# Decoding the picked experts with integers, and starting the gate groups one unit earlier

## The chip, the cores and the metric

The kernel runs on one core of one Trainium2 chip. The metric is the device time of one execution in microseconds (us), the median of the runs shown. The engines are named PE (TensorE), DVE (VectorE), ACT (ScalarE), POOL (GpSimd) and SP (SyncE, here only a DMA queue).

## The reference, cut to what matters

Two transformer blocks in fp32 over 256 tokens of width 2048. The change lies in the expert layer (PEER) of the first block:

```python
q = (t @ wq).reshape(T, 8, 2, 128)
s1, s2 = q[:, :, 0] . k1, q[:, :, 1] . k2            # 128 scores per head and half
v1, i1 = top_k(s1, 16);  v2, i2 = top_k(s2, 16)
cand = (v1[..., :, None] + v2[..., None, :])         # 16 x 16 sums
sc, pos = top_k(cand, 16)                            # slot = pos // 16, pos % 16
idx = i1[slot // 16] * 128 + i2[slot % 16]
g = softmax(sc)
out = sum_k g_k * gelu(u[idx_k] . t) * v[idx_k]
```

There are 8 heads with 16 picks each, so 128 picks a token. For each pick the kernel has a position of 0 to 255 in the 16 x 16 table; its upper four bits are a slot in the first list of keys, its lower four a slot in the second. Looking up which key (0 to 127) stands in that slot is called decoding here.

## The kernel before, in words

**The weight stream.** All large weights come as one stream of 532 units of 128x2048 fp32, loaded by SP into four raw buffers. Each unit is split into two fp32r parts so that PE keeps nearly fp32 precision: ACT copies it rounded (`w_hi`, line 672, the function `ahead` of ACT) and DVE subtracts that from the raw unit (`w_lo`, line 1117, `ahead` and `lo` of DVE). There are two buffers of each. ACT may write unit k+2 only when PE has finished unit k (`mm_done`); DVE may subtract only when ACT has written; PE may begin a unit only when DVE has subtracted (`split_done`). The next raw load into a slot starts when its unit is split. `ahead(u)` on ACT and on DVE prepares unit u+2.

**The expert layer.** It is computed densely for 208 of the 256 tokens. The first stages of the stream are `wq` (16 units, queries), `u0` and `u1` (16 units each, the scores of the experts 0 to 2047 and 2048 to 4095), then `e0` and `e1` (their outputs), and so on. A unit of `u0` or `u1` is 48 matmuls of 208 columns (lines 1884 to 1886). Beside `wq` and `u0` DVE does the top-k searches, and after them the decoding, lines 1482 to 1506, in which it places a `fill()` between its own steps: a `fill()` is the DVE half of `ahead` for the next unit of `u0`. For each half of the tokens (`tt`) DVE casts the key numbers to floats (`top_f`), cuts the positions into two slots (`posab`), casts those (`posf`), and then for each of the two lists (`half`) compares the slots with 0 to 15 (line 1499), multiplies the result by the key numbers (line 1502) and adds up over 16 (line 1506). Two more `fill()` follow, since six of the sixteen were placed in the search and eight in the decoding.

**The gates.** The softmax is begun by DVE (line 1492, `sm_dve`), its exponentials are ACT's (line 900). In ACT's order of work they stand behind all of `u0`, so behind the eviction of its last unit and behind the copy of `w_hi` for the second unit of `u1`. DVE then divides (lines 1511 to 1513) and signals `picks_done`. PE turns the picks by six transposes (`picks_turn`, line 2192), DVE copies them (lines 1523 and 1524) and builds one-hot tiles: for a gate group of four tokens `picks(q)` writes one `pick_b` (line 1532) and four `pick_a` (line 1537). PE multiplies them (`gate_group`, line 2203), ACT evicts the group into `stage` (line 909), and every fourth group is written to memory (line 913) and partly kept (line 916). There are 52 groups. `picks(q)` waits for the matmuls of group q-2. `GATES_UNIT` says which unit of `u1` holds which groups: five each in the units 1 to 10, two in unit 11. Within a unit PE puts them behind the steps kt = 2, 5, 8, 11 and 15 of its 16 (`GATES_AFTER`). DVE puts the `w_lo` of unit k+1 behind the second group of unit k. ACT, in unit k, evicts up to four groups, then waits for the end of the unit, evicts it with a Gelu (line 925), copies `w_hi` of unit k+2, and evicts the fifth group.

**Behind the gates.** When the last group is evicted, DVE weighs the activations of `u0` by the gates, four tiles at a time (`gated0`, lines 1555, 1567, 1570). `gated0(0)` also waits until the last even block of gates is written to memory. Only then comes the next `w_lo`, and after it `gated0(1)` and so on. Stage `e0` begins when all 16 units of `u1` are done.

Of the kernel before, what the change touches and what calls it, by code (L numbers as in the profile page):

```python
# [15 lines left out]
F32 = mybir.dt.float32  # L16
F32R = mybir.dt.float32r
U32 = mybir.dt.uint32
ACT = mybir.ActivationFunctionType
AX = mybir.AxisListType  # L20

P = 128
# [13 lines left out]
PEER_HEADS, PEER_KEYS, TOPK = 8, 128, 16  # L36
PICKS = PEER_HEADS * TOPK
# [90 lines left out]
def build(nc, x_in, mem_in, stream, cols_in, consts_in, rows_in, wide_in, wdtf_in, keys_in,  # L128
          rel_in, onehot_in, u_rows, v_rows, out):
    ctx = ExitStack()  # L130
    with ctx:
        base = [-(-nc.sbuf_base // 32) * 32]

        def at(name, shape, dt, offset):
            return nc.alloc_sbuf_tensor_at(name, shape, dt, offset=offset)
# [25 lines left out]
        work_at = base[0]  # L161
# [27 lines left out]
        def C(name, a=0, b=None):  # L189
            lo, hi = CONSTS[name]  # L190
            return consts[:, lo + a:(hi if b is None else lo + b)]
# [24 lines left out]
        act0 = at("act0", [P, KT, T], F32, work_at)  # L216
        wide = at("wide", [P, D], F32, work_at)
        cand = at("cand", [P, 2, TT, 256], F32, work_at + 24576)
        onehot = at("onehot", [P, PICKS, TOPK], F32, work_at + 24576)
        pick_a = at("pick_a", [P, 8, P], F32, work_at + 24576)  # L220
        pick_b = at("pick_b", [P, 8, P], F32, work_at + 28672)
        gbuf = at("gbuf", [P, 4, TBLOCKS, 4 * TBLOCK], F32, work_at + 16384)
        pk = work_at + 32768

        top_v = [at(f"top_v{tt}", [P, 16, TOPK], F32, o) for tt, o in enumerate((pk, wdtf_at))]
        top_i = [at(f"top_i{tt}", [P, 16, TOPK], U32, o + 1024) for tt, o in enumerate((pk, wdtf_at))]
        top_f = at("top_f", [P, 16, TOPK], F32, pk + 2048)
        sc = at("sc", [P, TT, PEER_HEADS, TOPK], F32, pk + 3072)
        pos = [at(f"pos{tt}", [P, PEER_HEADS, TOPK], U32, pk + o) for tt, o in enumerate((4096, 12928))]
        posab = at("posab", [P, 2, PICKS], U32, pk + 4608)  # L230
        posf = at("posf", [P, 2, PICKS], F32, pk + 5632)
        picked = at("picked", [P, TT, 3, PICKS], F32, pk + 6656)
        pickT = at("pickT", [P, 3, T], F32, pk + 9728)
        gsum = at("gsum", [P, TT, PEER_HEADS], F32, pk + 12800)
# [188 lines left out]

        GROUPS = TD // 4
        GATES_AFTER = (2, 5, 8, 11, 15)
        GATES_UNIT = {1 + q // 5: [n for n in range(GROUPS) if n // 5 == q // 5] for q in range(GROUPS)}

        LAST_GROUP = max(GATES_UNIT)

# [236 lines left out]
        def _(act):  # L666
# [253 lines left out]
            for k in range(16):  # L920
                u, groups = UNIT0["u1"] + k, GATES_UNIT.get(k, [])
                for q in groups[:4]:
# [187 lines left out]
        def _(dve):  # L1110
            eng = nc.vector
            own = Steps(eng, dve_own)
# [7 lines left out]
            def ahead(u, *loops):  # L1120
                lo(lin(u + 3, *loops), u + 2)
# [227 lines left out]
            for s in range(MIX_STEPS):  # L1349
# [11 lines left out]
                n = s - SSD_AT  # L1361
# [95 lines left out]
            waiting = [UNIT0["u0"] + j for j in range(16)]  # L1457

            def fill():
                ahead(waiting.pop(0))  # L1460
# [3 lines left out]
            for s in range(2 * PEER_HEADS + 6):  # L1464
                for k in range(2):
                    one, two = KEYS_AT.get(s - 1 - k), KEYS_AT.get(s - 3 - k)
# [11 lines left out]
                if s == 2:  # L1478
                    eng.wait_ge(s_wide2, 16)
                    eng.tensor_tensor(xw[0:G, :], x[0:G, 0, :], wide2[0:G, :], ALU.mult).then_inc(xw_done, 1)  # L1480

            for tt in range(TT):
                own.did(eng.tensor_copy(top_f[:, :, :], top_i[tt][:, :, :]))
                tf = top_f[:, :, :].rearrange("p (h two) k -> p h two k", two=2)

                own.did(eng.tensor_copy(first[:, :], sc[:, tt, :, 0]))

                pf = pos[tt][:, :, :].rearrange("p h k -> p (h k)")
                own.did(eng.tensor_scalar(posab[:, 0, :], pf, 4, None, ALU.logical_shift_right))
                own.did(eng.tensor_scalar(posab[:, 1, :], pf, 15, None, ALU.bitwise_and))  # L1490
                own.wait()
                eng.tensor_tensor(sc[:, tt, :, :], sc[:, tt, :, :],
                                  first[:, :].unsqueeze(2).to_broadcast([P, PEER_HEADS, TOPK]),
                                  ALU.subtract).then_inc(sm_dve, 1)
                own.do(eng.tensor_copy(posf[:, :, :], posab[:, :, :]))
                for half in range(2):
                    if waiting:
                        fill()
                    own.do(eng.tensor_tensor(onehot[:, :, :], C("iota", 0, TOPK).unsqueeze(1).to_broadcast([P, PICKS, TOPK]),
                                             posf[:, half, :].unsqueeze(2).to_broadcast([P, PICKS, TOPK]), ALU.is_equal))  # L1500
                    oh = onehot[:, :, :].rearrange("p (h k) a -> p h k a", h=PEER_HEADS)
                    own.do(eng.tensor_tensor(oh, oh, tf[:, :, half, :].unsqueeze(2).to_broadcast([P, PEER_HEADS, TOPK, TOPK]),
                                             ALU.mult))
                    if waiting:
                        fill()
                    own.do(eng.tensor_reduce(picked[:, tt, half, :], onehot[:, :, :], AX.X, ALU.add))
            while waiting:
                fill()
            for tt in range(TT):
                eng.wait_ge(sm_act, tt + 1)  # L1510
# [26 lines left out]
                    eng.tensor_scalar(pick_a[:, j + i, :], C("iota"), pickT[:, 0, t:t + 1], pickT[:, 2, t:t + 1],  # L1537
                                      ALU.is_equal, ALU.mult).then_inc(oha_done, 1)

            for k in range(1, LAST_GROUP + 1):  # L1540
                for n, q in enumerate(GATES_UNIT[k]):
                    if n == min(2, len(GATES_UNIT[k]) - 1):
                        ahead(UNIT0["u1"] + k - 1)
                    picks(q)
# [325 lines left out]
        def _(pe):  # L1870
            eng = nc.tensor
# [294 lines left out]
            for s in range(WQ_STEPS):  # L2166
                if s in KEYS_AT:
                    h = KEYS_AT[s]
# [17 lines left out]
            def picks_turn():  # L2186

                eng.wait_ge(picks_done, TT)
                for n in range(3):
                    for tt in range(TT):  # L2190
                        o = bank[6 + n // 2][:, (n % 2) * T + tt * P:(n % 2) * T + tt * P + P]
                        last = eng.transpose(o, picked[:, tt, n, :], C("ident"))
                last.then_inc(pickT_psum, 1)

            def gate_group(q):

                eng.wait_ge(ohb_done, q + 1)
                if q >= 4:
                    eng.wait_ge(g_evict, q - 3)
                for i in range(4):  # L2200
                    eng.wait_ge(oha_done, 4 * q + i + 1)
                    j = 4 * (q % 2) + i
                    mm(bank[4 + q % 4][:, i * P:i * P + P], pick_b[:, j, :], pick_a[:, j, :], start=True, stop=True)\
                        .then_inc(g_mm, 1)

            for k in range(16):
                groups = GATES_UNIT.get(k, [])

                def between(kt, groups=groups):
                    if kt in GATES_AFTER and GATES_AFTER.index(kt) < len(groups):  # L2210
                        gate_group(groups[GATES_AFTER.index(kt)])

                eng.wait_ge(split_done, UNIT0["u1"] + k + 1)
                eng.wait_ge(bank_free, 4 * ROUND0["u1"] + k + 1)
                if k == 1:
                    picks_turn()
                feature_unit(k, a1, between=between, c0=G)
            feature("e0", 16, None, unit=part_unit, tile=e0_pair, c1=TD, ready=lambda kt: eng.wait_ge(a2_ready, Z_TILES + kt + 1))
# [145 lines left out]
            for j in range(8, 16):  # L2364
# [5 lines left out]
                if j in (8, 9, 12):  # L2370
                    n = {8: 0, 9: 1, 12: 2}[j]
# [169 lines left out]
```

## Time and profile before

| what | value |
|---|---|
| time, median of 3 runs | 3111.43 us (3110.13 to 3116.72) |
| the profiled execution | 3117.25 us, of which the span of the profile is 3115.5 us |
| busy share of the span | PE 97%, DVE 72%, ACT 46%, POOL 6% |
| mean granted clock of PE | 0.99 of 2.4 GHz |
| `u0` ends, picks turned, first `pick_b` | 644.2, 650.6, 652.6 us |
| last `pick_a` ends, `e0` begins | 762.8, 789.1 us |

Times in the rows are microseconds from the start of the span. A row of a timeline gives start, duration, engine, line, operation, output<-input, shape, count, and in brackets the idle time of the engine before it with what ended that. A row of the stretches gives, for each engine, busy time and (instructions), and then the granted clock of PE as a share of 2.4 GHz, the busy share of the DMA engines and GB/s.

### The profile page before, as it was taken

What the parts mean: (1) busy time and instruction counts of PE and PEld (TensorE: products, weight loads), DVE (VectorE), ACT (ScalarE), POOL (GpSimd) and SP (SyncE); (2) the same over time, 40 slices, a digit from 0 to 9 for tenths busy, and PEclk for the clock granted to TensorE, in tenths of its full rate; (3) what the DMA queues carried; (4) which work ended last, traced back from release to release, by engine and by line L of the source; (5) the groups of instructions that cost most, each with busy time, mean ns of one, the idle gap of its engine ahead of it and who ended that gap; (6) DMA issues with size and microseconds to landing.
All of it is one profiled execution on the core that took longest, in us unless ns stands there. A gap on an engine that the chain in (4) does not pass through costs nothing. (4 is left out here: it accounts for less than half of the span.)

```text
span 3115.5 us, 49787 instructions
## 1 busy us (share of the span) xinstructions
PE 3019.5 (97%) x19428; PEld 2808.5 (90%) x19428; DVE 2258.5 (72%) x3201; ACT 1426.0 (46%) x1762; POOL 180.1 (6%) x223
## 2 busy tenths in 40 slices
PE   7999999999997999999999999999999999999998
PEld 7899889999997999999999999999788888888886
DVE  4766559999865889888988877598656646555564
ACT  4465443356443444555454455434444333333333
POOL 1000000020000111111111100000000000000000
PEclk9999999999998999999999999999999999999999
DMA  5443464456768999999999874544444555555553
GB/s 204 175 149 136 150 211 150 166 199 229 255 252 227 339 343 354 342 352 343 356 338 359 315 294 179 182 177 150 162 176 148 185 194 188 189 188 188 188 188 135
DMA packets 101661, 705.49 MB, mean 226 GB/s; under 512 B 13320, under 2 KB 13344, under 8 KB 17728
## 3 DMA queue, kind: packets, MB, share of 16 engines
q1 hardware_dynamic: 77472, 562.07, 50.0%
q0 software_dynamic: 22192, 128.10, 11.9%
q10 hardware_dynamic: 1872, 13.63, 1.1%
q8 instruction: 80, 1.31, 0.2%
q14 instruction: 45, 0.37, 0.0%
HBM read 685.46 MB, written 18.24 MB: 226 GB/s over the span
## 5 line engine op out<-in xcount | busy, mean ns | idle before, releaser
L1117 DVE TENSOR_TENSOR w_lo<-raw,w_hi 128x2048 fp32r<-128x2048 f32 x532 | 1218.5, 2290 | 514.8 <-ACT w_hi L672 489.6
L1906 PE MATMUL bank<-a_both,w_hi 128*128 128x416 f32 (+1 forms) x3840 | 1231.0, 378 | 25.5 <-DVE w_lo L1117 21.8
L1907 PE MATMUL bank<-a_both,w_lo 128*128 128x208 f32 (+1 forms) x4096 | 1042.8, 265 | 0.0
L1906 PEld LDWEIGHTS bank<-a_both,w_hi 128*128 128x128 f32 x3840 | 725.5, 189 | 80.9 <-issue 25.7
L1907 PEld LDWEIGHTS bank<-a_both,w_lo 128*128 128x128 f32 x4096 | 782.6, 191 | 7.2
L672 ACT ACTIVATE w_hi<-raw 128x2048 fp32r<-128x2048 f32 x308 | 588.4, 1911 | 379.8 <-PE bank L1938 361.6
L1884 PE MATMUL bank<-a_both,w_hi 128*128 128x256 f32 (+1 forms) x1984 | 572.9, 289 | 21.0 <-DVE w_lo L1117 13.7
L685 ACT ACTIVATE w_hi<-raw 128x1536 fp32r<-128x1536 f32 x224 | 333.7, 1490 | 523.2 <-PE bank L1907 503.7
L1885 PE MATMUL bank<-a_both,w_hi 128*128 128x256 f32 (+1 forms) x1984 | 560.0, 282 | 0.0
L1886 PE MATMUL bank<-a_both,w_lo 128*128 128x256 f32 (+1 forms) x1984 | 559.9, 282 | 0.0
L1884 PEld LDWEIGHTS bank<-a_both,w_hi 128*128 128x128 f32 x1984 | 383.7, 193 | 28.9 <-issue 11.1
L1885 PEld LDWEIGHTS bank<-a_both,w_hi 128*128 128x128 f32 x1984 | 383.9, 193 | 0.5
L1886 PEld LDWEIGHTS bank<-a_both,w_lo 128*128 128x128 f32 x1984 | 383.5, 193 | 0.0
L1936 PE MATMUL bank<-w_hi,a_both 128*128 128x512 f32 x960 | 377.6, 393 | 2.0 <-DVE a_both L1128 1.5
L1938 PE MATMUL bank<-w_hi,a_both 128*128 128x512 f32 x960 | 373.9, 389 | 0.0
L1937 PE MATMUL bank<-w_lo,a_both 128*128 128x512 f32 x960 | 373.6, 389 | 0.0
L1936 PEld LDWEIGHTS bank<-w_hi,a_both 128*128 128x128 f32 x960 | 180.2, 188 | 40.6 <-DVE a_both L1128 2.2
L1938 PEld LDWEIGHTS bank<-w_hi,a_both 128*128 128x128 f32 x960 | 180.2, 188 | 37.9
L1937 PEld LDWEIGHTS bank<-w_lo,a_both 128*128 128x128 f32 x960 | 180.3, 188 | 36.3
L1906 PE MATMUL bank<-e_both,w_hi 128*128 128x416 f32 x480 | 146.0, 367 | 0.0
L691 ACT ACTIVATE w_hi<-raw 128x512 fp32r<-128x512 f32 x224 | 138.3, 617 | 0.0
L1907 PE MATMUL bank<-e_both,w_lo 128*128 128x208 f32 x512 | 127.1, 258 | 0.0
(327 smaller groups left out, 2529.3 us busy)
## 6 DMA issues: line engine op xcount, KB each, us to landing
raw<-stream_dram SPq DMA_DIRECT2D x532, 1024.0 KB, 4.9
gates_scratch<-stage ACTq DMA_DIRECT2D x13, 1024.0 KB, 4.4
gbuf<-gates_scratch POOLq DMA_DIRECT2D x30, 416.0 KB, 7.3
x<-x_dram SPq DMA_DIRECT2D x2, 1024.0 KB, 6.5
x_scratch<-x POOLq DMA_DIRECT2D x1, 2048.0 KB, 11.0
set_rows<-xw_scratch POOLq DMA_DIRECT2D x2, 1024.0 KB, 22.9
mem<-mem_dram POOLq DMA_DIRECT2D x1, 2048.0 KB, 9.7
xm<-x_scratch POOLq DMA_DIRECT2D x1, 2048.0 KB, 12.5
```

The lines of the kernel that those rows point to most:

```text
L672: eng.activation(w_hi[k % SPLIT][:, :], raw[:, k % RAW, :], ACT.Copy).then_inc(hi_done, 1)
L685: eng.activation(w_hi[k % SPLIT][:, 0:PART], raw[:, k % RAW, 0:PART], ACT.Copy)
L691: eng.activation(w_hi[k % SPLIT][:, PART:UNIT], raw[:, k % RAW, PART:UNIT], ACT.Copy).then_inc(hi_done, 1)
L1117: eng.tensor_tensor(w_lo[k % SPLIT][:, :], raw[:, k % RAW, :], w_hi[k % SPLIT][:, :].bitcast(F32), ALU.subtract).then_inc(split_done, 1)
L1884: mm(o, hi[:, ks], tile(0, kt), start=kt == 0, stop=False)
L1885: mm(o, hi[:, ks], tile(1, kt), start=False, stop=False)
L1886: last = mm(o, lo[:, ks], tile(0, kt), start=False, stop=kt == KT - 1)
L1906: mm(o, hi[:, ks], pair, start=kt == 0, stop=False)
L1907: inst = mm(o2, lo[:, ks], pair[:, 0, :], start=False, stop=False, skip_group_check=True)
L1936: mm(o, tile(0, k0 + k)[:, ts], hi[:, ns], start=first and k == 0, stop=False)
L1937: mm(o, tile(0, k0 + k)[:, ts], lo[:, ns], start=False, stop=False)
L1938: last = mm(o, tile(1, k0 + k)[:, ts], hi[:, ns], start=False, stop=end and k == 3)
```

## The change

The decoding is done in integers. Each key number gets its own slot number above it (`slot * 128` or'ed on, `top_x`), the slots wanted are shifted left by seven bits in the instruction that cuts them out, and an exclusive-or of the two gives the bare key number where the slots agree and at least 128 where they don't; a minimum over sixteen leaves the key number. So the multiplication over 2048 elements and the cast `posf` fall away, and one small instruction that makes the slot numbers comes in.

The gate groups begin one unit earlier: three in unit 0 of `u1` (behind kt = 8, 11, 15), five each in the units 1 to 9, four in unit 10. The picks are turned ahead of unit 0 instead of unit 1. One `fill()` is left over in `waiting` and never taken from it: the `w_lo` of unit 1 of `u1` is now written behind the second gate group, by the loop over the groups, which starts at k = 0.

```diff
-        onehot = at("onehot", [P, PICKS, TOPK], F32, work_at + 24576)
+        differ = at("differ", [P, PICKS, TOPK], U32, work_at + 24576)
-        top_f = at("top_f", [P, 16, TOPK], F32, pk + 2048)
+        top_x = at("top_x", [P, 16, TOPK], U32, pk + 2048)
-        posf = at("posf", [P, 2, PICKS], F32, pk + 5632)
+        slot_x = at("slot_x", [P, TOPK], U32, pk + 5632)
...
-        GATES_UNIT = {1 + q // 5: [n for n in range(GROUPS) if n // 5 == q // 5] for q in range(GROUPS)}
+        GATES_UNIT = {(q + 2) // 5: [n for n in range(GROUPS) if (n + 2) // 5 == (q + 2) // 5] for q in range(GROUPS)}
...
+            own.do(eng.tensor_scalar(slot_x[:, :], C("iota", 0, TOPK), float(PEER_KEYS), None, ALU.mult))
             for tt in range(TT):
-                own.did(eng.tensor_copy(top_f[:, :, :], top_i[tt][:, :, :]))
-                tf = top_f[:, :, :].rearrange("p (h two) k -> p h two k", two=2)
+                own.did(eng.tensor_tensor(top_x[:, :, :], top_i[tt][:, :, :],
+                                          slot_x[:, :].unsqueeze(1).to_broadcast([P, 16, TOPK]), ALU.bitwise_or))
+                tx = top_x[:, :, :].rearrange("p (h two) k -> p h two k", two=2)
...
-                own.did(eng.tensor_scalar(posab[:, 0, :], pf, 4, None, ALU.logical_shift_right))
-                own.did(eng.tensor_scalar(posab[:, 1, :], pf, 15, None, ALU.bitwise_and))
+                own.did(eng.tensor_scalar(posab[:, 0, :], pf, 4, 7, ALU.logical_shift_right, ALU.logical_shift_left))
+                own.did(eng.tensor_scalar(posab[:, 1, :], pf, 15, 7, ALU.bitwise_and, ALU.logical_shift_left))
...
-                own.do(eng.tensor_copy(posf[:, :, :], posab[:, :, :]))
                 for half in range(2):
                     if waiting:
                         fill()
-                    own.do(eng.tensor_tensor(onehot[:, :, :], C("iota", 0, TOPK).unsqueeze(1).to_broadcast([P, PICKS, TOPK]),
-                                             posf[:, half, :].unsqueeze(2).to_broadcast([P, PICKS, TOPK]), ALU.is_equal))
-                    oh = onehot[:, :, :].rearrange("p (h k) a -> p h k a", h=PEER_HEADS)
-                    own.do(eng.tensor_tensor(oh, oh, tf[:, :, half, :].unsqueeze(2).to_broadcast([P, PEER_HEADS, TOPK, TOPK]),
-                                             ALU.mult))
+                    own.do(eng.tensor_tensor(
+                        differ[:, :, :].rearrange("p (h k) a -> p h k a", h=PEER_HEADS),
+                        posab[:, half, :].rearrange("p (h k) -> p h k", h=PEER_HEADS).unsqueeze(3)
+                        .to_broadcast([P, PEER_HEADS, TOPK, TOPK]),
+                        tx[:, :, half, :].unsqueeze(2).to_broadcast([P, PEER_HEADS, TOPK, TOPK]), ALU.bitwise_xor))
                     if waiting:
                         fill()
-                    own.do(eng.tensor_reduce(picked[:, tt, half, :], onehot[:, :, :], AX.X, ALU.add))
-            while waiting:
+                    own.do(eng.tensor_reduce(picked[:, tt, half, :], differ[:, :, :], AX.X, ALU.min))
+            while len(waiting) > 1:
                 fill()
...
-            for k in range(1, LAST_GROUP + 1):
+            for k in range(LAST_GROUP + 1):
...
-                def between(kt, groups=groups):
-                    if kt in GATES_AFTER and GATES_AFTER.index(kt) < len(groups):
-                        gate_group(groups[GATES_AFTER.index(kt)])
+                places = GATES_AFTER if k else GATES_AFTER[-len(groups):]
+
+                def between(kt, groups=groups, places=places):
+                    if kt in places and places.index(kt) < len(groups):
+                        gate_group(groups[places.index(kt)])
...
-                if k == 1:
+                if k == 0:
                     picks_turn()
```

## Rows read from the trace of the kernel before

**Rows 1.** The page: busy time of each engine over the span.
```profile
PE 3019.5 (97%) x19428; PEld 2808.5 (90%) x19428; DVE 2258.5 (72%) x3201; ACT 1426.0 (46%) x1762; POOL 180.1 (6%) x223
```

**Rows 2.** The stretches: the gates, and from the last group to `e0`.
```profile
651.20:762.10 110.90, 104.26 (x909) 102.46 (x907) 109.47 (x271) 77.95 (x84) 17.74 (x36) 1.00 0.59 218
762.10:789.10 27.00, 25.99 (x230) 25.85 (x231) 22.00 (x55) 9.95 (x10) 7.00 (x6) 1.00 0.87 278
```

**Rows 3.** The timeline of DVE: one half of the decoding and its cast.
```profile
591.68 0.28 DVE L1495 CAST posf<-posab 128x256 f32<-128x256 uint32 x1
...
596.42 2.28 DVE L1499 TENSOR_TENSOR onehot<-consts,posf 128x2048 f32<-128x2048 f32 x1
598.74 2.29 DVE L1502 TENSOR_TENSOR onehot<-onehot,top_f 128x2048 f32<-128x2048 f32 x1
601.07 2.29 DVE L1117 TENSOR_TENSOR w_lo<-raw,w_hi 128x2048 fp32r<-128x2048 f32 x1
603.27 2.28 DVE L1506 TENSOR_REDUCE picked<-onehot 128x128 f32<-128x2048 f32 x1
```

**Rows 4.** The timeline of ACT: evictions of units 7, 8 and 15 of `u0`.
```profile
597.33 0.34 ACT L894 ACTIVATE act<-bank 128x208 f32<-128x208 f32 x1 [3.22 <-PE bank L1886]
...
602.68 0.34 ACT L894 ACTIVATE act<-bank 128x208 f32<-128x208 f32 x1 [3.21 <-PE bank L1886]
...
644.48 0.34 ACT L894 ACTIVATE act<-bank 128x208 f32<-128x208 f32 x1 [3.87 <-PE bank L1886]
```

**Rows 5.** The timeline of PE: the longest of five late unit starts.
```profile
627.46 0.36 PE L1884 MATMUL bank<-a_both,w_hi 128*128 128x208 f32 x1 [1.25 <-DVE w_lo L1117]
```

**Rows 6.** The timeline of ACT behind that eviction: the exponentials.
```profile
644.72 1.91 ACT L672 ACTIVATE w_hi<-raw 128x2048 fp32r<-128x2048 f32 x1
646.64 1.28 ACT L900 ACT_TABLE_LOAD   x1
647.94 0.51 ACT L900 ACTIVATE sc<-sc 128x128 f32<-128x128 f32 x2
```

**Rows 7.** The timeline of DVE: softmax, copies, first two groups.
```profile
648.87 0.28 DVE L1511 TENSOR_REDUCE gsum<-sc 128x8 f32<-128x128 f32 x1
...
651.50 0.69 DVE L1523 COPY pickT<-bank 128x512 f32<-128x512 f32 x1 [0.58 <-PE bank L2192]
...
652.55 0.69 DVE L1532 TENSOR_TENSOR pick_b<-consts,pickT 128x512 f32<-128x512 f32 x1
...
654.18 0.69 DVE L1532 TENSOR_TENSOR pick_b<-consts,pickT 128x512 f32<-128x512 f32 x1
```

**Rows 8.** The timeline of PE: the turn of the picks.
```profile
650.61 0.85 PE L2192 MATMUL bank<-consts,picked 128*128 128x128 f32 x6 [0.81 <-DVE picked L1513]
```

**Rows 9.** The timeline of PE: a longer wait.
```profile
560.75 0.54 PE L1884 MATMUL bank<-a_both,w_hi 128*128 128x208 f32 x1 [2.88 <-DVE w_lo L1117]
```

**Rows 10.** The stretch behind this wait, and one behind another wait.
```profile
560.70:566.70 6.00, 5.95 (x28) 5.96 (x29) 5.93 (x21) 0.00 (x0) 0.00 (x0) 0.50 0.50 178
...
1932.30:1935.40 3.10, 3.10 (x16) 3.10 (x16) 3.10 (x3) 0.00 (x0) 0.00 (x0) 0.50 0.74 259
```

**Rows 11.** The timeline of ACT: one group is evicted.
```profile
660.31 1.06 ACT L909 ACTIVATE stage<-bank 128x512 f32<-128x512 f32 x1 [2.47 <-PE bank L2203]
```

**Rows 12.** The timeline of DVE behind the last group.
```profile
761.66 1.11 DVE L1537 TENSOR_SCALAR pick_a<-consts,pickT 128x128 f32<-128x128 f32 x4
765.14 1.23 DVE L1555 TENSOR_TENSOR act<-act,gbuf 128x208 f32<-128x208 f32 x4 [2.37 <-ACT gbuf L916]
768.65 0.80 DVE L1567 CAST e_both<-act 128x208 fp32r<-128x208 f32 x4 [2.27 <-DMA gates_scratch<-stage]
...
770.63 2.28 DVE L1117 TENSOR_TENSOR w_lo<-raw,w_hi 128x2048 fp32r<-128x2048 f32 x1
```

**Rows 13.** The timeline of PE: unit 13 of `u1`, and the first matmul of `e0`.
```profile
772.97 0.37 PE L1884 MATMUL bank<-a_both,w_hi 128*128 128x208 f32 x1 [0.96 <-DVE w_lo L1117]
...
789.14 0.42 PE L1906 MATMUL bank<-e_both,w_hi 128*128 128x416 f32 x1
```

## The prediction

> **What bounds the kernel now.** The page comes first: PE is busy for 97% of the span [rows 1], so a change on DVE pays only where PE waits for DVE. The stretches come next: between the turn of the picks and the last gate group DVE is busy for 109.5 of 110.9 us [rows 2], so there DVE sets the pace and PE waits a little in each unit. Then the timelines around the change. In the decoding the unit starts of `u0` are late: an unhindered unit takes 5.35 us (597.33 to 602.68), but the last seven take 41.8 us (602.68 to 644.48) instead of 37.4 [rows 4]. So 4.4 us are lost, in five late starts, the longest of which waits 1.25 us for `w_lo` [rows 5]. Behind the last group the chain is another: group evicted, written to memory, activations weighed, and only then the next `w_lo` [rows 12]. The view of ACT matters as well: the exponentials come behind the last unit's eviction and a `w_hi` [rows 6].
>
> **The change, step by step.** The sum is made against the profiled execution (3117.25 us, span 3115.5); that is 5.8 us over the median of 3111.43, and I carry the difference over to the median.
>
> *Decoding.* Four multiplications of 2.29 us fall away with their gaps (598.74 to 601.07, 2.33 each), so 9.3 us, and two casts of about 0.3 [rows 3]; one small instruction (0.2) comes in. DVE has 9.7 us less to do. The exclusive-or over 2048 uint32 is not in the trace, nor is the minimum. I take the 2.28 us of the comparison and of the sum, of the same shape. Lower bound: 1.9 us, ACT's pass over 2048 [rows 6], which changes nothing, as will be seen; upper bound: 4.6 us, as much as comparison and multiplication together [rows 3]. The or over 256 elements and the double shifts go by the cast and by the instructions that they replace, a tenth more or less.
> What it is worth: per two units of `u0` DVE then has two `w_lo` (2 x 2.2) and two passes (2 x 2.3), 9.0 us against PE's 10.7. The late starts go, PE is the bound, and the last eviction moves from 644.48 to 640.1: **-4.4 us**. More cannot come of it, for a faster DVE now waits for `w_hi`. About half of the 9.7 us ends as idle time.
>
> *The turn of the picks.* It now stands ahead of unit 0 of `u1`, so PE has nothing to do from the end of `u0` until `picks_done`. From the last eviction to the first exponential done it is 3.8 us (644.48 to 648.2), which doesn't shrink [rows 6]: 643.9. From DVE's `gsum` to the turn it is 1.74 us (648.87 to 650.61) [rows 7, 8]: the turn starts at 645.7 (650.61 before), after 5.6 us without work on PE; before, unit 0 filled this time and the wait was 0.81 [rows 8]. A wait of 2.88 us was followed by 6.0 us at a granted clock of 0.50, another by at least 3.1 [rows 9, 10]; so after 5.6 us I expect the 1.2 GHz level for 3.1 to 6 us, middle 4.7, in which PE loses half. The six transposes then take 0.5 more. First `pick_b`: 645.7 + 1.9 + 0.5 = 648.1 against 652.55 [rows 7], again **-4.4**.
>
> *The groups of unit 0.* From here to the last `pick_a` (762.77) DVE did 52 groups of 1.63 and eleven `w_lo` [rows 7, 12]; now it is the same number, unit 1's in place of unit 12's. What is added is idle time. The `w_hi` of unit 2 waits on ACT behind three evictions, the third of a group that PE reaches only behind kt = 15. DVE has the first five groups and one `w_lo` out at 648.1 + 8.2 + 2.2 = 658.5, of which 0.5 is held back by PE's matmuls at most. The third group ends on PE near 657.1; eviction 1.1 [rows 11], table load 1.3, Gelu 0.3, `w_hi` 1.9 [rows 6]: 661.7. DVE stands for 2.7 us. PE then waits 3.4 us for group 5, the clock falls a second time, and DVE waits some 2.0 us for slow matmuls (`picks` stays within two groups of PE). With 0.2 of the 0.5, idle time is 4.9 us where it was 1.1: **+3.8**. The last `pick_a` ends 0.6 us earlier than before, at 762.2.
>
> *Behind the last group.* Before, the `w_lo` that follows the weighing was unit 13's: 762.77 to the unit's start at 772.97 is 10.2 us, with 0.96 of wait, and three units lead to `e0` at 789.14 [rows 12, 13]. Now the last group is in unit 10, and the `w_lo` behind the same chain is unit 12's. The 10.2 us stay, and four units follow: **+5.4 us**. PE has only a quarter of unit 10 and unit 11 to fill it (6.7 us), waits about 3.4, and by rows 9 and 10 the clock falls again: half of 4.7, **+2.4**.
>
> *What is hidden.* POOL's copies of the indices and gates start 4 us earlier and are wanted in `e0`; without that lead they would still be early. ACT's gate writes and POOL's loads of them keep their distance to the last group. SP's raw load into the slot of unit 1 starts later, since that unit is split in the gates; its data are wanted four units on.
>
> **Sum:** -4.4 + 3.8 + 5.4 + 2.4 = **+7.2 us** at the start of `e0`, and nothing behind it is bound to anything but PE's progress. Profiled: 3124.5; median: 3111.4 + 7.2 = **3118.6 us**. With slow stretches of 3.1 us each it is +5.2, with 6 us +9.3.
>
> **A rule against the rows.** From the table load to the first exponential there are 1.30 us, of which the load is 1.28 [rows 6]: nothing stands between. The Trainium skill (ScalarE: Activation LUTs, "What ACT_TABLE_LOAD costs") has a drain of about 1.38 us behind each switch. By that page both loads on the new path would cost more, and the sum would be about +10; the trace disagrees.
>
> **The rivals.**
> 1. *The clock stays up.* Same path, no loss of clock. For it: the gates and what follows them ran at a granted clock of 1.00 before [rows 2]; against it: they held no wait as long, and rows 9 and 10 show what follows one. The start of `pick_b` gains 0.5, DVE idles 2.0 instead of 4.9: -4.9 + 0.9 + 5.4 = +1.4 to 1.6, median 3113.0.
> 2. *Faster: the decoding is worth all it frees.* Place: DVE between 596 and 763, full to 99% in the gates [rows 2]. If the exponentials came before DVE is through with the decoding, each microsecond off DVE would be one off the end: -9.7, median 3101.7. It decides at the turn: it must start by 641 instead of 645.7, and the unit more behind the last group must be covered. ACT's order speaks against it.
> 3. *The integers are dear.* A pass at the upper bound costs DVE 2.3 x 4 = 9.2 us more, the late starts of `u0` come back, the -4.4 is gone: +11.6, median 3123. Against it: the cast from uint32 takes 0.28 us for 256 elements, 1.1 ns each, and the float passes 2.28 for 2048, 1.1 as well [rows 3].
> 4. *A drain behind the load.* If ACT needed another 1.3 us (once more the load's time) behind each of the two loads: +2.6, so +9.8, median 3121.2. Against it: the 0.02 us of rows 6. That is the page's rule above.
> 5. *It is evened out.* `e0` starts later, but a later wait for DMA shrinks, or single executions differ by more than the change (the three runs span 6.6 us): within 0.2%.
>
> **How the numbers follow.** A measurement of this kernel can tell about 0.2%, 6.2 us, from no change. Forecast 0.50 (three quarters of it beyond 6.2: 0.38 slower, 0.12 same); rival 1 0.12 (same); rival 2 0.17 (faster); rival 3 0.04 and rival 4 0.03 (slower); rival 5 0.14 (same). So slower 0.45, within 0.2% 0.38, faster 0.17. The range takes in rivals 1, 3, 4 and 5 and leaves out rival 2 and a little above: 3107 to 3123. The forecast's own range is 3116.6 to 3120.7.
>
> **What would show it.** Right: the last unit of `u0` evicted near 640, no late start in the decoding; a wait of 5 to 6 us on PE ahead of line 2192, released by DVE's `picked`, with clock 0.50 behind it; DVE idle ahead of the third `w_lo` of `u1`, released by ACT; last `pick_a` near 762; unit 12 waiting 3 us or more for `w_lo`; `e0` at 794 to 798. Wrong: the turn before 643, `e0` before 788, or an exclusive-or over 3 us.

## The result, and the profile after

The changed kernel takes **3117.89 us** (median of 20 runs, 3113.62 to 3122.74), the kernel before beside it on the same chips 3112.68 us (20 runs). The ratio is **1.0018, with a 95% interval of 1.0011 to 1.0025**: some 5.2 us slower. The profiled execution of the changed kernel took 3116.12 us, with a span of 3114.3 us. Of the experiments below, e5 and e7 each had one far longer execution (10959.96 and 3269.56 us), which their medians below include and their ratios leave out.

The page, busy time of each engine. DVE has 8.8 us less to do than in [rows 1] (9.7 were forecast, gaps between instructions included), and PE is as busy as before.

```profile
PE 3015.8 (97%) x19428; PEld 2809.0 (90%) x19428; DVE 2249.7 (72%) x3196; ACT 1425.7 (46%) x1762; POOL 179.9 (6%) x223
```

The timeline of DVE in the decoding (start, duration, engine, line, operation, names, shape, count, and in brackets the idle time before it with what ended that). The new passes at lines 1500 and 1507 last as long as the float passes in [rows 3]. One of the three is gone, and DVE now waits for `w_hi` in its place.

```profile
590.50 0.17 DVE L1482 TENSOR_SCALAR slot_x<-consts 128x16 uint32<-128x16 f32 x1
590.70 0.43 DVE L1484 TENSOR_TENSOR top_x<-top_i,slot_x 128x256 uint32<-128x256 uint32 x1
...
595.79 2.28 DVE L1500 TENSOR_TENSOR differ<-posab,top_x 128x2048 uint32<-128x2048 uint32 x1
599.36 2.29 DVE L1117 TENSOR_TENSOR w_lo<-raw,w_hi 128x2048 fp32r<-128x2048 f32 x1 [1.29 <-ACT w_hi L672]
601.57 2.28 DVE L1507 TENSOR_REDUCE picked<-differ 128x128 f32<-128x2048 uint32 x1
```

The timeline of ACT: the last eviction of `u0` stands at 639.64 (644.48 in [rows 4]). The exponentials come 3.5 us behind it, and the first Gelu and `w_hi` of unit 2 behind the third gate group.

```profile
639.64 0.34 ACT L894 ACTIVATE act<-bank 128x208 f32<-128x208 f32 x1 [3.22 <-PE bank L1887]
639.88 1.90 ACT L672 ACTIVATE w_hi<-raw 128x2048 fp32r<-128x2048 f32 x1
641.80 1.28 ACT L900 ACT_TABLE_LOAD   x1
643.10 0.51 ACT L900 ACTIVATE sc<-sc 128x128 f32<-128x128 f32 x2
...
656.05 1.08 ACT L909 ACTIVATE stage<-bank 128x512 f32<-128x512 f32 x1 [1.16 <-PE bank L2204]
657.16 1.28 ACT L925 ACT_TABLE_LOAD   x1
658.45 0.34 ACT L925 ACTIVATE act<-bank 128x208 f32<-128x208 f32 x1
658.69 1.90 ACT L672 ACTIVATE w_hi<-raw 128x2048 fp32r<-128x2048 f32 x1
```

The timeline of DVE from the exponentials on, those rows ahead of which it was idle. The last three waits before the `...` are one for ACT's `w_hi`, ahead of the third `w_lo`, and two for PE's slow matmuls from group 5 on. They are the price of the earlier groups.

```profile
643.44 0.29 DVE L1512 TENSOR_REDUCE gsum<-sc 128x8 f32<-128x128 f32 x1 [4.62 <-ACT sc L900]
646.74 0.69 DVE L1524 COPY pickT<-bank 128x512 f32<-128x512 f32 x1 [1.25 <-PE bank L2193]
660.63 2.29 DVE L1117 TENSOR_TENSOR w_lo<-raw,w_hi 128x2048 fp32r<-128x2048 f32 x1 [2.39 <-ACT w_hi L672]
669.63 0.69 DVE L1533 TENSOR_TENSOR pick_b<-consts,pickT 128x512 f32<-128x512 f32 x1 [1.83 <-PE bank L2204]
671.99 0.69 DVE L1533 TENSOR_TENSOR pick_b<-consts,pickT 128x512 f32<-128x512 f32 x1 [0.64 <-PE bank L2204]
...
760.80 1.10 DVE L1538 TENSOR_SCALAR pick_a<-consts,pickT 128x128 f32<-128x128 f32 x4
764.54 1.23 DVE L1556 TENSOR_TENSOR act<-act,gbuf 128x208 f32<-128x208 f32 x4 [2.64 <-ACT gbuf L916]
```

The timeline of PE, its three long waits in the changed stretch and the first matmul of `e0`. Before, the waits at the turn and behind the last group were 0.81 [rows 8] and 0.96 us, those within the gates 1.72 at most, and `e0` began at 789.14 [rows 13].

```profile
645.19 1.52 PE L2193 MATMUL bank<-consts,picked 128*128 128x128 f32 x6 [5.58 <-DVE picked L1514]
663.92 0.98 PE L2204 MATMUL bank<-pick_a,pick_b 128*128 128x128 f32 x3 [3.12 <-DVE pick_a L1538]
772.05 0.50 PE L1885 MATMUL bank<-a_both,w_hi 128*128 128x208 f32 x1 [2.65 <-DVE w_lo L1117]
795.21 0.37 PE L1907 MATMUL bank<-e_both,w_hi 128*128 128x416 f32 x1
```

The stretches of the changed kernel behind these three waits, and between the first `pick_b` and the last `pick_a`. The columns are window, length, busy time of PE, weight loads, DVE, ACT and POOL with (instructions), then PE's granted clock, the DMA share and GB/s. Behind each wait PE ran at the 1.2 GHz level, for 3.9, 5.5 and 3.4 us.

```profile
645.20:649.10 3.90, 3.90 (x19) 3.90 (x20) 2.58 (x8) 0.00 (x0) 3.32 (x7) 0.50 0.03 4
663.90:669.40 5.50, 5.48 (x26) 5.50 (x27) 3.90 (x13) 1.08 (x1) 0.00 (x0) 0.50 0.77 270
772.00:775.40 3.40, 3.35 (x16) 3.35 (x17) 3.37 (x13) 0.00 (x0) 1.14 (x1) 0.52 0.96 213
...
647.80:761.90 114.10, 108.75 (x922) 107.28 (x922) 109.24 (x271) 78.40 (x84) 15.50 (x32) 0.96 0.58 208
```

The same stretch of the kernel before, in the same columns: the same 271 instructions of DVE, the same work, and 3.9 us less.

```profile
652.55:762.77 110.22, 103.63 (x902) 102.04 (x903) 109.12 (x271) 77.17 (x83) 16.39 (x34) 1.00 0.59 214
```

### The profile page after: what moved, and what is told of

Same layout as the page of the kernel before. It is cut to its first block and busy times, and to the rows that moved or that the text cites. A ratio compares the mean times of both kernels' runs of the same rounds, so it can differ in the third digit from the quotient of the medians.

```text
span 3114.3 us, 49780 instructions
## 1 busy us (share of the span) xinstructions
PE 3015.8 (97%) x19428; PEld 2809.0 (90%) x19428; DVE 2249.7 (72%) x3196; ACT 1425.7 (46%) x1762; POOL 179.9 (6%) x223
```

## The experiments

Ten kernels ran, nine of them variants. The times are medians of 11 or 12 runs, each beside runs of the kernel before on the same chips (3112.23, 3112.57 and 3112.85 us for the three sets in which they ran). The other columns are read from one profile each, in us. Differences of medians across sets, as given below, are up to 2 us larger or smaller than the ratios make them.

| kernel | ratio to before, 95% interval | time | first `pick_b` | last `pick_a` ends | `e0` |
|---|---|---|---|---|---|
| before | | | 652.55 | 762.77 | 789.14 |
| the change | 1.0018 (1.0011 to 1.0025) | 3117.89 | 647.80 | 761.90 | 795.21 |
| e1, decoding only | 0.9990 (0.9981 to 0.9998) | 3109.28 | 647.53 | 757.73 | 784.52 |
| e2, earlier groups only | 1.0022 (1.0013 to 1.0031) | 3119.43 | 652.62 | 766.20 | 797.94 |
| e3, all waits filled | 1.0003 (0.9994 to 1.0011) | 3112.61 | 647.65 | 758.59 | 791.21 |
| e4, exponentials earlier | 0.9992 (0.9983 to 1.0001) | 3108.88 | 643.84 | 753.32 | 788.31 |
| e5, `w_lo` ahead of casts | 1.0009 (1.0000 to 1.0019) | 3116.12 | 648.31 | 762.33 | 795.31 |
| e6, e4 and e5 together | 0.9982 (0.9974 to 0.9991) | 3107.70 | 643.08 | 752.56 | 785.59 |
| e7, only the turn's wait filled | 1.0011 (1.0002 to 1.0020) | 3115.90 | 647.28 | 759.74 | 794.43 |
| e8, the kernel before again | | 3106.03 (one execution) | 651.96 | 762.17 | 788.92 |
| e9, decoding and exponentials | 0.9985 (0.9975 to 0.9994) | 3108.29 | 647.76 | 757.96 | 784.74 |
| e10, e6 with one wait filled | 0.9979 (0.9970 to 0.9987) | 3106.57 | 642.87 | 752.32 | 783.76 |

Single executions also lie apart ahead of the changed stretch. The last eviction of `u0` stands at 639.45 to 640.29 with the integer decoding, but at 641.05 in e4, which was 1.4 us behind the changed kernel before the decoding began (an eviction at 582.09 instead of 580.68). Differences of the last three columns below 1 us say little.

**e1: the decoding alone.** The changed kernel with the places of the groups turned back.

```diff
-        GATES_UNIT = {(q + 2) // 5: [n for n in range(GROUPS) if (n + 2) // 5 == (q + 2) // 5] for q in range(GROUPS)}
+        GATES_UNIT = {1 + q // 5: [n for n in range(GROUPS) if n // 5 == q // 5] for q in range(GROUPS)}
...
-            while len(waiting) > 1:
+            while waiting:
...
-            for k in range(LAST_GROUP + 1):
+            for k in range(1, LAST_GROUP + 1):
...
-                if k == 0:
+                if k == 1:
                     picks_turn()
```

> Integer decoding alone, the gate groups and the turn where they were before. Theory A (the decoding takes the late starts out of u0 and is worth 4.4 us, all of the harm is in the move): last unit of u0 evicted 4 to 4.5 us earlier, the turn, the last pick_a and e0 as well; time 4.4 us under the kernel before. Rival B (DVE sets the pace right through, so each microsecond off DVE is one off the end): 9.7 us under. Rival C (the decoding brings nothing that lasts, what it gains is lost in later waits for DMA): within 2 us of before.

It is about 3 us faster than the kernel before. Its first `pick_b` is 5.0 us earlier, of which this execution was ahead by 0.8 us early in the decoding (an eviction of `u0` at 591.21 instead of 591.97), and `e0` 4.6 us. So 8.8 us less work on DVE (the page above) turned into 4 to 5 us at `e0` in this execution, and 3 us (0.6 to 5.9) in the median, no more.

**e2: the earlier groups alone.** The kernel before with those lines moved forward, and its float decoding.

```diff
-            while waiting:
+            while len(waiting) > 1:
...
-            for k in range(1, LAST_GROUP + 1):
+            for k in range(LAST_GROUP + 1):
...
-                if k == 1:
+                if k == 0:
                     picks_turn()
```

> Float decoding as before, turn and gate groups one unit earlier. Theory A (the move costs one unit behind the last group, 5.4, idle time on DVE of some 4, and 2 of clock, and doesn't depend on the decoding): wait of 5.6 us ahead of the turn as with both, e0 11 us later than before, time 10 to 11 us over before. Rival B (the move pays once DVE is less loaded and only harms a loaded DVE; the parts interact): over 13 us above before. Rival C (the move is neutral): within 2 us of before.

This is the slowest of all, 0.22% over the kernel before. The two halves add up: -0.10% and +0.22% give +0.12%, and the change has +0.18% (0.11 to 0.25). So the loss is that of the moved groups, and the decoding gives part of it back. Two waits of PE in this kernel, and the stretches behind them in the columns given above:

```profile
669.45 0.77 PE L2203 MATMUL bank<-pick_a,pick_b 128*128 128x128 f32 x2 [3.10 <-DVE pick_a L1537]
...
776.42 0.37 PE L1884 MATMUL bank<-a_both,w_hi 128*128 128x208 f32 x1 [2.72 <-DVE w_lo L1117]
```

```profile
776.40:780.00 3.60, 3.58 (x32) 3.59 (x33) 3.57 (x13) 0.00 (x0) 1.14 (x1) 1.00 1.00 223
669.40:673.00 3.60, 3.55 (x18) 3.58 (x19) 3.60 (x13) 1.07 (x1) 0.00 (x0) 0.55 0.98 335
```

The clock fell behind the first and stayed at 1.00 behind the second, though that wait is longer than the 2.65 us behind which it fell in the changed kernel. `e0` stands 31.7 us behind the last `pick_a`, against 33.3 in the changed kernel: the difference of 1.6 us is what the fall costs there, in these two executions.

**e3 and e7: the waits filled.** Matmuls whose result is overwritten keep PE busy while it would wait. In e3 they stand ahead of the turn, ahead of group 5 (eight, by a line of `gate_group` like those below) and ahead of unit 12; e7 has only the first of the three. The added instructions compute nothing that is used.

```diff
+            BUSY = {0: 14, 12: 8}
+
+            def busy(k, n):
+                for _ in range(n):
+                    mm(bank[k % 4][:, 0:TD], C("ident"), C("tri", 0, TD), start=True, stop=True)
...
                 eng.wait_ge(bank_free, 4 * ROUND0["u1"] + k + 1)
+                if k in BUSY:
+                    busy(k, BUSY[k])
                 eng.wait_ge(split_done, UNIT0["u1"] + k + 1)
```

> The change, and on PE extra matmuls whose result is overwritten, in the three long waits: 14 ahead of the turn, 8 ahead of group 5, 8 ahead of unit 12. Nothing else is different. Theory A (the clock that falls in these waits costs about 5 us at e0: 1 behind the turn, 2.4 behind group 5, 1.7 behind unit 12): granted clock 1.00 from 645 to 795, e0 at 790 instead of 795.2, time 5 us under the change and 0.5 to 1.5 over before. Rival B (the clock costs nothing since DVE sets the pace): e0 at 795, same time as the change. Rival C (extra matmuls delay PE by themselves): later than the change.

The granted clock is 1.00 from 640 to 798, the timeline and the stretch of e3:

```profile
639.96 5.10 PE L2200 MATMUL bank<-consts 128*128 128x208 f32 x28
645.70 0.85 PE L2193 MATMUL bank<-consts,picked 128*128 128x128 f32 x6 [0.65 <-DVE picked L1514]
```

```profile
640.00:798.00 158.00, 153.52 (x1297) 151.01 (x1296) 139.60 (x338) 98.50 (x105) 24.68 (x42) 1.00 0.62 218
```

The last `pick_a` ends 3.3 us earlier than in the changed kernel, `e0` begins 4.0 us earlier and the time is 5.3 us less. This is the clock's share, and the kernel is then level with the one before. What is left is the unit more behind the last group: `e0` stands 32.6 us behind the last `pick_a`, where the kernel before has 26.4. Of these 6.2 us the unit is 5.4; the rest is unit 12 starting 11.05 us behind the last `pick_a` instead of 10.15, since DVE waited 2.83 us for the gates to be written (1.95 in the changed kernel).

> The change with extra matmuls on PE only in the wait ahead of the turn (14, result overwritten). Theory A (the clock that falls there costs 1 us at e0, since DVE idles more than half of it anyway; most of the 5 us of all three waits comes from the other two): granted clock 1.00 from 645 to 660, first pick_b and last pick_a 1 us earlier or less, the wait at group 5 as before, time 1 us under the change. Rival B (that wait is the one that costs): 3 us or more under the change.

The turn alone is worth 0.5 us at the first `pick_b` and 2.2 us at the last `pick_a`, where 1 us at most was expected. The median is 2.0 us under that of the changed kernel, and the intervals overlap. At unit 12 the wait is then 3.01 us, and the 5 us from 770 on ran at a clock of 0.50, so that `e0` comes only 0.8 us earlier. A gain ahead of a wait lengthens the wait.

**e4: the exponentials earlier.** ACT's two exponentials stand behind the `w_hi` of the last unit of `u0` instead of behind all of `u0`.

```diff
                         if k > 0:
                             ahead(u0 + k, (r, RU))
+                        if k == 13 and name == "u0":
+                            exps()
...
-            for tt in range(TT):
-                eng.wait_ge(sm_dve, tt + 1)
-                eng.activation(sc[:, tt, :, :], sc[:, tt, :, :], ACT.Exp).then_inc(sm_act, 1)
```

> The change, with the two exponentials moved on ACT from behind u0 to behind the w_hi that follows unit 13 of u0. Theory A (the turn waits for the exponentials, which stand behind the last unit of u0 on ACT): wait ahead of the turn 1 us instead of 5.6, no fall of the clock there, last pick_a 9 us earlier than in the change, e0 at 785 to 786, time 9 us under the change and 3 to 4 under before. Rival B (the turn waits for DVE, not for ACT): wait unchanged. Rival C (the table loads now delay the evictions and w_hi of u0): u0 ends later by 1 us or more and half of the gain goes.

The turn starts at 641.90, behind a wait of 0.89 us, instead of at 645.19 behind 5.58. The two table loads among the evictions delay nothing: from the first eviction named above to the last of `u0` it is 58.96 us in both kernels. The last `pick_a` ends 8.6 us earlier than in the changed kernel, more than the turn gained, since the waits of DVE and the falls of the clock in the first units are gone too (PE waits 1.63 us for group 5, at 1.00). The time is 9.0 us under that of the changed kernel. `e0` at 788.31 is later than the 785 to 786 expected: the execution started 1.4 us behind, and 3.0 us are lost at unit 12, the timeline of PE there and the stretch behind:

```profile
763.76 0.54 PE L1887 MATMUL bank<-a_both,w_hi 128*128 128x208 f32 x1 [2.93 <-DVE w_lo L1119]
```

```profile
763.70:771.00 7.30, 7.24 (x38) 7.25 (x38) 7.23 (x23) 0.00 (x0) 1.68 (x2) 0.56 1.02 286
```

**e5 and e6: the `w_lo` of unit 12 ahead of the casts.** e5 is the changed kernel with this edit, e6 has that of e4 as well.

```diff
                 for j in range(4):
                     weigh(act0[:, 4 * g + j, 0:TD], g, j)
+                if g == 0:
+                    ahead(u1 + LAST_GROUP)
...
             for k in range(LAST_GROUP, 16):
-                ahead(u1 + k)
+                if k > LAST_GROUP:
+                    ahead(u1 + k)
```

> The change, with one order changed on DVE behind the last group: the w_lo of unit 12 is written between the weighing of the first four tiles and their casts, instead of behind them. Theory A (behind the last group PE waits for unit 12 because its w_lo stands behind the write of the gates to memory): no wait at unit 12 and no fall of the clock there, 1.5 to 2 us of wait at unit 13 instead, e0 at 792 instead of 795.2, time 3 us under the change, 2 over before. Rival B (PE would have waited for w_hi or DMA at that place anyway): wait unchanged, same time as the change.

> The change with both: the exponentials early on ACT, and the w_lo of unit 12 ahead of the casts. Theory A (the two waits are separate terms of the sum and both can be had): last pick_a at 753, e0 at 782 to 784, time 5 to 7 us under before, so faster than the integer decoding alone (3.0 under). Rival B (behind the gates DVE is the bound, so that the second gives nothing more): e0 at 786 or later, time as with the early exponentials alone, 3.4 under before.

The `w_lo` of unit 12 begins 4.7 us behind the last `pick_a` instead of 7.8, since it no longer waits for the gates to be written. ACT's `w_hi` is in time for it but for 0.81 us, the timeline of DVE in e5:

```profile
764.99 1.23 DVE L1556 TENSOR_TENSOR act<-act,gbuf 128x208 f32<-128x208 f32 x4 [2.66 <-ACT gbuf L916]
767.03 2.29 DVE L1117 TENSOR_TENSOR w_lo<-raw,w_hi 128x2048 fp32r<-128x2048 f32 x1 [0.81 <-ACT w_hi L672]
769.24 1.64 DVE L1572 CAST e_both<-act 128x208 fp32r<-128x208 f32 x4
...
775.18 2.29 DVE L1117 TENSOR_TENSOR w_lo<-raw,w_hi 128x2048 fp32r<-128x2048 f32 x1
```

But the next `w_lo` stands behind two blocks of weighing, at 775.18, and so PE waits ahead of unit 13 instead of unit 12, up to 777.52 for 2.33 us, with 3.4 us at a clock of 0.61 behind it. `e0` is 33.0 us behind the last `pick_a`, against 33.3: the wait moved on by a unit, and the 3 us expected of this edit did not come. The median is 1.8 us under that of the changed kernel, within the intervals. With the earlier exponentials (e6) the time is 3107.70 us, faster than the kernel before and the changed one. `e0` is 2.7 us earlier than in e4, at 785.59 and not at 782 to 784, and the median 1.2 us lower, but the intervals of the two overlap.

**e8: the kernel before once more**, unchanged, for a second profile.

> The kernel before, unchanged, profiled a second time. Theory A (what differs behind e0 between the profiles, 1061.7 us from e0 to the norm of the memory in the kernel before and 1052.9 to 1059.7 in the others, is scatter of the DMA waits near 970 to 1050): u0, turn, gates and e0 within 1 us of the first profile, the stretch behind e0 differs by 2 us or more. Rival B (a later e0 makes these waits shorter): the stretch behind e0 is 1061 to 1062 again.

This single execution took 3106.03 us, with a span of 3104.2. Up to the last `pick_a` it is a steady 0.6 us ahead of the first profile (762.17 and 762.77), as it was in `u0` (602.08 and 602.68), and at `e0` 0.2 us (788.92 and 789.14). In between its clock fell, behind the last group, where that of the first profile did not. The timeline of PE and the stretch behind, in e8:

```profile
761.55 1.66 PE L2203 MATMUL bank<-pick_a,pick_b 128*128 128x128 f32 x8 [1.72 <-DVE pick_a L1537]
...
761.50:764.50 3.00, 2.95 (x16) 2.98 (x17) 0.67 (x3) 1.05 (x1) 0.00 (x0) 0.58 0.89 303
```

The same in the first profile of the same kernel, with the same wait:

```profile
762.15 1.17 PE L2203 MATMUL bank<-pick_a,pick_b 128*128 128x128 f32 x8 [1.72 <-DVE pick_a L1537]
...
762.10:765.00 2.90, 2.85 (x25) 2.88 (x26) 0.67 (x3) 1.24 (x2) 0.00 (x0) 1.00 0.89 305
```

Behind `e0` the two part: to the norm of the memory it is 1051.2 us, against 1061.7. The timeline of PE in e8:

```profile
987.67 0.71 PE L1906 MATMUL bank<-a_both,w_hi 128*128 128x416 f32 x1 [8.42 <-DVE w_lo L1117]
```

In the first profile:

```profile
990.94 0.71 PE L1906 MATMUL bank<-a_both,w_hi 128*128 128x416 f32 x1 [11.20 <-DVE w_lo L1117]
```

So a pair of profiles says nothing on the stretch behind `e0`. The changed kernel's span is 1.2 us shorter than that of the first profile although its `e0` is 6.1 us later; the medians show the loss.

**e9: the decoding and the earlier exponentials, the groups where they were.**

> The integer decoding with the exponentials at their earlier place, but with the gate groups where the kernel before has them (five a unit from unit 1, the picks turned ahead of unit 1). Theory (the earlier groups have no worth of their own: DVE sets the pace from the first pick_b on, and they only give up cover in front of it and behind it): the picks are ready at about 642, unit 0 of u1 runs on PE up to 645.5 or so, the turn comes behind it or between, first pick_b near 647, last pick_a near 757, and behind it the old distance of 26.5 us: e0 near 784, the time 3 to 4 us under the kernel before, the same as the decoding alone, and 0 to 1 us off the version with all changes. Rival (the early exponentials pay only together with the early groups): the decoding alone had its turn at 645.6 for its place behind unit 0, so nothing moves here either; e0 at 784.5, and the versions with early groups and early exponentials (e0 at 785.6 and 788.3) are as good. The two agree on e0 and differ from a third: that the early exponentials free DVE and bring the turn before 643, e0 at 780, 3104.

`e0` begins at 784.74, as in e1, and the time is 1.0 us under that of e1, inside both intervals. The early exponentials alone move nothing, as both theories of the expectation had it. The reason is the one that its rival gives: the turn stands behind unit 0, and PE stood idle ahead of it for only 0.81 us, so earlier picks could gain no more. The timeline of DVE shows what held the picks even for these:

```profile
641.87 2.29 DVE L1119 TENSOR_TENSOR w_lo<-raw,w_hi 128x2048 fp32r<-128x2048 f32 x1 [3.00 <-ACT w_hi L672]
644.08 0.28 DVE L1514 TENSOR_REDUCE gsum<-sc 128x8 f32<-128x128 f32 x1
```

Without the moved groups the `w_lo` of the second unit of `u1` is a `fill()` ahead of `gsum`, and it waits 3.00 us for `w_hi`. The change does both at once, it turns the picks ahead of unit 0 and leaves this `fill()` to the loop over the groups, and with both the early exponentials pay (e4). No run has one without the other.

**e10: e6 with the wait filled**, by five matmuls whose result is overwritten, ahead of unit 12 (`BUSY = {12: 5}`). The wait of e6 is, as in e5, one unit further on, so unit 12 comes 2 us later and the wait of 2.37 us shrinks to 0.68.

> The change with the exponentials earlier, the w_lo of unit 12 ahead of the casts, and five idle matmuls (2 us, their result is overwritten) on PE in its wait ahead of unit 12. Theory (a fallen clock costs there what the records of PE show, some 3.8 us at half speed in the version without these matmuls): the clock stays at 1.00, e0 stands 31 us behind the last pick_a instead of 33.0, and the time is 1.5 to 2 us under that version's 3107.7, so 3106. Rival (the loss is given back at the waits of 5 to 9 us further on, near 975 and 990): e0 comes 2 us earlier and the time is the same, within 1 us of 3107.7, those waits longer by 2 us in all.

`e0` stands 31.4 us behind the last `pick_a` instead of 33.0. From 764 to 784 the clock is 1.00, where e6 had 3.8 us at 0.55 behind a wait of 2.37, the stretch of e6:

```profile
767.70:771.50 3.80, 3.71 (x18) 3.71 (x19) 3.77 (x14) 0.00 (x0) 1.14 (x1) 0.55 1.08 228
```

and of e10:

```profile
764.00:784.00 20.00, 19.32 (x173) 19.17 (x172) 16.29 (x33) 6.49 (x7) 3.03 (x3) 1.00 0.97 297
```

The waits near 970 and 985 are 15.2 us in sum, in e6 15.6, so this pair shows nothing given back there, though by e8 one pair can't settle it. The time of 3106.57 us is the lowest median, 0.21% under the kernel before. It is 1.1 us under that of e6, but the intervals overlap, so it is not shown that the 1.6 us reach the end.

## Why the prediction was right, step by step

The forecast was 3118.6 us, slower by 7.2; measured were 3117.89 us and 5.2 more. It lies in the range and in the forecast's own range. The ratio's interval (1.0011 to 1.0025) excludes no difference, so it is slower. By the bound that the text set (0.2%) the ratio of 1.0018 is on its edge, inside it, so the chance of 0.38 for no difference met it as much as the 0.45 for slower: this measurement is good to 0.07% either way, finer than the text assumed.

- **The decoding, -4.4.** Right in cause, and in size within what single executions allow (-4.8 against the first profile of the kernel before, -4.2 against e8): the last unit of `u0` was evicted at 639.64 (640.1 foretold), and the new passes took the 2.28 us taken for them. The or over 256 elements took 0.43 us, the cast that it replaces 0.29. e1 shows the step alone, with 4.6 us at `e0`. A good half of DVE's lead ends as idle time: it waits 6.0 us in sum for `w_hi`, ahead of seven `w_lo` from 599 to 639 (the first is shown above), where before it had no such wait.
- **The turn.** A wait of 5.58 (5.6), then the clock at 0.50 for 3.9 us (3.1 to 6, middle 4.7), six transposes in 1.52 us instead of 0.85; first `pick_b` at 647.80 (648.1).
- **The groups, +3.8.** 114.10 against 110.22 us, so +3.9. DVE is idle for 4.86 us of it (4.9 foretold): 2.39 us for the `w_hi` of unit 2 (2.7), then 1.83 and 0.64 for slow matmuls (2.0). PE waited 3.12 us for group 5 (3.4). Last `pick_a` at 761.90 (762.2).
- **Behind the last group, +5.4.** From the last `pick_a` to the unit's start it is 10.15 us (10.2 before), with four units behind it instead of three: this term came as foretold. e2 shows it without a loss of clock behind unit 12: 31.7 us from the last `pick_a` to `e0`, and 26.4 before.
- **The clock at unit 12, +2.4.** Mis-sized. PE still had 7.5 us of work behind the last `pick_a` (up to 769.40), not 6.7, so it waited 2.65 us and not 3.4. It then ran 3.4 us at 0.52 instead of 4.7, which costs 1.6 us: the four units took 23.16 us, and three took 16.17, so 7.0 more, of which 5.4 is the unit. As a term it is also the least certain: by the same sum (from the unit's start to `e0`, less four times 5.39) the clock cost nothing in e2 and 3.0 us in e4. It was foretold from a row with a wait of 2.88 us; that the clock fell here, behind 2.65 us, and not in e2, behind 2.72, is in part luck.
- **The sum, +7.2 at `e0`.** 795.21 against 789.14 is +6.1, 0.8 of the difference from the clock at unit 12. The changed kernel's execution was also 0.6 us ahead at an early unit of the decoding (602.12 against 602.68), as e8 was (602.08).

**The rivals.** That the clock stays up was priced at +1.5 (3113.0); e3 is that case, made by hand, and came to 3112.61. That the decoding is worth all it frees (3101.7) is refuted by e1; it named ACT's order as what stands against it, and e4 shows that this order costs the changed kernel 9.0 us. e9 adds that with the turn in its old place, behind unit 0, early exponentials move nothing, and that a `fill()` ahead of `gsum` holds the picks there as well, which the prediction did not name. Dear integers are refuted by the 2.28 us of both passes. The drain behind a load is refuted by the rows of ACT: from a load's start to the next activation it is 1.30 us at 641.80 and 1.29 at 657.16, of which the load is 1.28. The Trainium skill (ScalarE: Activation LUTs, "What ACT_TABLE_LOAD costs") has about 1.38 us more there, and this trace again disagrees. That it is evened out (rival 5) is refuted for the median, by an interval of 3.4 to 7.8 us more; its second half holds for single profiles, as e8 shows.

**Open** is why PE's clock falls behind one wait and not behind another of the same length, even in two executions of one kernel (e8). It was not isolated.

## What to carry to other kernels

Starting work earlier pays only if what it waits for is earlier too: here the groups moved ahead of the unit that had covered the exponentials, and the wait, the slow clock behind it and one more unit behind the last group cost more than the decoding saved. When an engine off the critical path gets faster, follow its next wait in the queue order of the engine that feeds it; moving two exponentials (e4) was worth 9.0 us on the changed kernel, where 9 us less work on DVE (e1) was worth 3. And profile the same kernel twice before reading a pair of profiles: here two executions of one kernel differ by 0.6 us up to the last gate group, by a fall of the clock behind it, and by 10 us in the rest.

## What the hardware showed that was not expected

The clock's fall is no function of the wait's length alone, nor of the kernel. PE kept 1.00 behind a wait of 2.72 us (e2), and fell behind waits of 2.65 us (the change, 3.4 us at 0.52) and 2.93 us (e4, 7.3 us at 0.56). In the kernel before a wait of 1.72 us ahead of the last group left the clock at 1.00 in the whole stretch [rows 2]. In a second execution of that kernel (e8, the rows above) the same wait was followed by a fall, and so it was in e1 and e9, before the same group, in e1 the timeline and the stretches:

```profile
757.11 1.17 PE L2204 MATMUL bank<-pick_a,pick_b 128*128 128x128 f32 x8 [1.72 <-DVE pick_a L1538]
```

```profile
758.00:761.00 3.00, 3.00 (x20) 3.00 (x18) 0.89 (x4) 1.36 (x2) 0.00 (x0) 0.61 0.95 399
761.00:762.00 1.00, 1.00 (x6) 1.00 (x6) 0.34 (x2) 0.00 (x0) 0.00 (x0) 0.50 0.98 418
762.00:763.00 1.00, 1.00 (x11) 1.00 (x10) 0.00 (x0) 0.00 (x0) 0.00 (x0) 0.96 0.89 377
```

Matmuls whose result is thrown away kept the clock at 1.00 wherever they filled the wait (e3, e10). The median of e3 is 5.3 us under that of the changed kernel; whether they also delay something, such as the write of the gates for which DVE waited 0.9 us longer in e3, is not shown.
